# The first stage of a two-block kernel, rearranged by pairs of feature blocks

## The chip, the core and the metric

The kernel runs on one core of one Trainium2 chip. The metric is device time in microseconds (us), the median of several executions. A core has five engines: TensorE (PE; its weight loads, PEld, overlap the matmuls), VectorE (DVE), ScalarE (ACT), GpSimd (POOL) and SyncE (SP), which only issues transfers here. All data are 32-bit floats, so that a matmul of 512 columns shows as two records in the trace.

## What is computed

Two transformer-like blocks run one after the other. The change touches the beginning of the first one, which in the reference is (cut):

```python
sh, sc, gt = jnp.split(jax.nn.silu(c) @ w_ada[l] + b_ada[l], 3, axis=-1)
sh_c, sc_c, gt_c = jnp.split(jax.nn.silu(c_ctx) @ w_ada[l] + b_ada[l], 3, axis=-1)
h = rms_norm(x, norm_g[l]) * (1 + sc[:, None]) + sh[:, None]
hc = rms_norm(ctx, norm_g[l]) * (1 + sc_c) + sh_c
qa, ka, va, ga, qb, kb, vb, gb, qn, kn, vn, gn = split_proj(h @ w_in[l])
```

x has 1024 tokens and ctx 256, each of 1024 features. Tokens are normalised, scaled and shifted per feature (the modulation, whose shift and scale come from a product of a small vector with the large matrix w_ada), and then projected.

## The kernel before, in words

Tokens lie in ten tiles of 128 (NT; eight of x, two of ctx), features in eight blocks of 128 (KC). A kernel is a row of stages; each is a block in which the five engines run their own programs and wait for each other by semaphores, and at its end all engines meet. An engine works through its program in order, so that whatever stands behind a wait waits too.

`stage_begin` (L270) is the first stage. Its parts, with the lines of the profile:

- Transfers: SP issues small parameters (L286), the even token tiles (L288) and two of the four adaLN jobs (L290: 2 MB each, 512 columns of w_ada); POOL issues the odd tiles (L301), ACT the two other jobs (L333). When all four jobs have landed, SP loads the first two chunks of w_in (L203), and POOL the rest of the constants (L304).
- Norm: ACT squares and sums each tile (`square`, L313), in two groups of five (HALF). DVE and ACT make the reciprocal root of a group (L368, L221, L222, L225 to L228), and DVE scales each tile (L373).
- Turning: PE transposes a scaled tile, eight transposes in two PSUM banks (`turn`, L400); DVE copies the first four feature blocks to hT (`put`, L360), ACT the last four (`keep`, L322).
- Modulation: for each job PE makes rows (`rows`, L263), DVE copies them (`keep_rows`, L356), PE turns them into columns (`columns`, L413). When all four are done, DVE adds bias and gain in two small steps (L381, L382). Then DVE (five feature blocks, L389) and ACT (three, L345) modulate all of hT in place, in three spans of tokens.
- Ten filler matmuls (`keep_busy`, L255; 20 records) stand on PE between the columns and the first projection.
- One unit of the projection (BEGUN = 1): eight matmuls of 512 columns (L432), for token tile 0, with chunk 0 of w_in.

The second stage, `stage_project_turned`, does the attention's first projection: ten units of 512 columns (one for each token tile), then ten copies of 256 columns with chunk 1. Its matmuls are at L1003. The first `ahead` units (BEGUN of them) have been made before, and PE only signals them. A unit is squared by ACT (L1079), normalised by DVE (L1174 to L1184), rotated by POOL (L1276 to L1285), and transposed by PE (L956) four units later. Four PSUM banks, 0, 1, 6 and 7, hold units in turn, so that unit 4 needs the bank of unit 0: PE waits until unit 0 has been normalised (`bank_read`). ACT loads its table at the stage's start (L1030).

The order of work on every engine is written out by hand; no planner sets it.

Of the kernel before, what the change touches and what calls it, by code (L numbers as in the profile page):

```python
# [266 lines left out]
BEGUN = 1  # L267


def stage_begin(pr, t, const_src, x_rows, loads, ada_src):  # L270
# [4 lines left out]
    JOBS = 4  # L275
    ORDER = (0, 2, 3, 1)
    HALF = NT // 2
    SOON = P + 2
    cols = ps[:, 6, 0:32].rearrange("p (b w) -> p b w", w=2)
    spans = [(0, 0, BANK), (0, BANK, SEQ), (1, SEQ, SEQ + CTX)]  # L280
    by_dve, by_act = range(0, 5), range(5, KC)
    with nc.Block() as block:
        @block.sync
        def _(sp):
            for n, (dst, src) in enumerate(loads):
                sp.dma_start(dst, src).then_inc(*S["params_in"].inc(16))  # L286
            for i in range(0, NT, 2):
                sp.dma_start(big[:, i, :], x_rows(i)).then_inc(*S[f"x_in_{i}"].inc(16))  # L288
            for n in range(2):
                sp.dma_start(adaw[:, n], ada_src(n)).then_inc(*S[f"ada_in_{n}"].inc(16))  # L290
            for n in range(JOBS):
                sp.wait_ge(*S[f"ada_in_{n}"](16))
            for i in range(SLOTS):
                pr.load(sp, i)

        @block.gpsimd
        def _(pool):
            pool.memset(cs[:], 0.0).then_inc(*S["cs_zero"].inc())
            pool.dma_start(t["const"][:, 0:SOON], const_src[:, 0:SOON]).then_inc(*S["const_in"].inc(16))
            for i in range(1, NT, 2):  # L300
                pool.dma_start(big[:, i, :], x_rows(i)).then_inc(*S[f"x_odd_in_{i}"].inc(16))  # L301
            for n in range(JOBS):
                pool.wait_ge(*S[f"ada_in_{n}"](16))
# [4 lines left out]
        def _(act):  # L308
            step = chained(act, S["act"])

            def square(i):
                act.wait_ge(*S[f"x_odd_in_{i}" if i % 2 else f"x_in_{i}"](16))
                step(act.activation(junk[:, 0:D], big[:, i, :], ACT.Square, accum_out=ssq[:, i:i + 1]))  # L313

            def root(g):
                act.wait_ge(*S["v_ready"](g + 1))
                at = slice(g * HALF, (g + 1) * HALF)
                pr.rsqrt_act(act, step, rs[:, at], ssq[:, at]).then_inc(*S["e_ready"].inc())

            def keep(i):  # L320
                act.wait_ge(*S["turned_1"](i + 1))
                act.activation(hT[:, 4:8, i * P:(i + 1) * P], ps[:, 2 * (i % 2) + 1, :].rearrange("p (k n) -> p k n", k=4),  # L322
                               ACT.Copy).then_inc(*S["kept_1"].inc())

# [5 lines left out]
            for i in range(HALF):  # L330
                square(i)
            for n in range(2, JOBS):
                act.dma_start(adaw[:, n], ada_src(n)).then_inc(*S[f"ada_in_{n}"].inc(16))  # L333
            root(0)
            for i in range(HALF):
                square(HALF + i)
                keep(i)
            root(1)
            for i in range(HALF, NT):
                keep(i)  # L340
            act.wait_ge(*S["mod_ready"](1))
            act.wait_ge(*S["kept_1"](NT))
            for w, a, b in spans:
                for k in by_act:
                    ins = act.activation(hT[:, k, a:b], hT[:, k, a:b], ACT.Identity, scale=mod[:, 0, 8 + k, w:w + 1], bias=mod[:, 0, k, w:w + 1])  # L345
                ins.then_inc(*S["modulated_act"].inc())

        @block.vector
        def _(dve):
            step = chained(dve, S["dve"])  # L350

            def keep_rows(j):
                dve.wait_ge(*S["rows_done"](j + 1))
                if j >= 2:
                    dve.wait_ge(*S["cols_done"](j - 1))
                dve.tensor_copy(row[:, j % 2, :], ps[:, 4 + j % 2, :]).then_inc(*S["rows_kept"].inc())  # L356

            def put(i):
                dve.wait_ge(*S["turned_0"](i + 1))
                dve.tensor_copy(hT[:, 0:4, i * P:(i + 1) * P], ps[:, 2 * (i % 2), :].rearrange("p (k n) -> p k n", k=4))\  # L360
                   .then_inc(*S["kept_0"].inc())

            dve.wait_ge(*S["params_in"](16 * len(loads)))
            parameters_dve(pr, dve, step, 0, t)
            for g in range(2):
                at = slice(g * HALF, (g + 1) * HALF)
                dve.wait_ge(*S["act"](HALF + g * (HALF + 1)))
# [4 lines left out]
                for i in range(g * HALF, (g + 1) * HALF):  # L372
                    dve.tensor_scalar(big[:, i, :], big[:, i, :], rs[:, i:i + 1], None, ALU.mult).then_inc(*S["xn_ready"].inc())  # L373
                    if i % HALF:
                        put(i - 1)
                put((g + 1) * HALF - 1)
            for j in range(JOBS):
                keep_rows(j)
            dve.wait_ge(*S["cols_done"](JOBS))
            m0 = mod[:, 0, 0:16, :]  # L380
            step(dve.tensor_tensor(m0, cols, spread(mods[:, 0, 8:24], [P, 16, 2], 2), ALU.add))  # L381
            dve.scalar_tensor_tensor(out=mod[:, 0, 8:16, :], in0=mod[:, 0, 8:16, :], scalar=1.0, in1=spread(mods[:, 0, 0:8], [P, 8, 2], 2),  # L382
                                     op0=ALU.add, op1=ALU.mult).then_inc(*S["mod_ready"].inc())
            dve.wait_ge(*S["mod_ready"](1))
            dve.wait_ge(*S["kept_0"](NT))
            dve.wait_ge(*S["kept_1"](NT))
            for w, a, b in spans:
                for k in by_dve:
                    ins = dve.tensor_scalar(hT[:, k, a:b], hT[:, k, a:b], mod[:, 0, 8 + k, w:w + 1], mod[:, 0, k, w:w + 1], ALU.mult, ALU.add)  # L389
                ins.then_inc(*S["modulated_dve"].inc())  # L390

        @block.tensor
        def _(pe):
            def turn(i):
                pe.wait_ge(*S["xn_ready"](i + 1))
                for h in range(2):
                    if i >= 2:
                        pe.wait_ge(*S[f"kept_{h}"](i - 1))
                    for k in range(4):
                        mm = pe.transpose(ps[:, 2 * (i % 2) + h, k * P:(k + 1) * P],  # L400
# [3 lines left out]
            def rows(j):  # L404
                pe.wait_ge(*S[f"ada_in_{ORDER[j]}"](16))
                if j >= 2:
# [3907 lines left out]
```

## Time and profile before

| | us |
|---|---|
| median of 3 executions | 3650.55 (3649.99 to 3651.01) |
| the profiled execution, its own time | 3654.28 |
| its span (first to last instruction) | 3652.5 |
| PE busy | 3533.3 (97% of the span) |
| DVE, ACT, POOL busy | 2282.5, 1269.1, 1044.2 |

The page of the profile gives busy time and groups of instructions for the whole span; the trace behind it is read by views: windows (busy time of each engine in a stretch, the granted TensorE clock and what the transfers did), the timeline of one engine, groups by line, and one line's instructions. Each time starts from the span's start. A line of a timeline merges neighbours of one kind: start, length to the end of the last one, and the count.

### The profile page before, as it was taken

The numbers are of one execution on the slowest core, as the hardware profiler recorded it, in microseconds if no ns is written. First come the engines' busy times: TensorE is split into PE (matmuls) and PEld (weight loads), VectorE is DVE, ScalarE is ACT, GpSimd is POOL, SyncE is SP. The second block draws the span as 40 slices with busy tenths as digits, with TensorE's granted clock in tenths as the row PEclk, the third lists the DMA queues.
The fourth block names the chain that finished last, engine by engine and source line by source line (L and its number), as shares of the span: only waits on it lengthen the run. The fifth ranks groups of instructions, "written<-read, shape, count | busy, mean of one in ns | idle before, by whom it ended". The sixth has DMA issues, their size and how long they took to land. (4 is left out here: it accounts for less than half of the span.)

```text
span 3652.5 us, 53885 instructions
## 1 busy us (share of the span) xinstructions
PE 3533.3 (97%) x20756; PEld 2540.0 (70%) x20756; DVE 2282.5 (62%) x4223; ACT 1269.1 (35%) x2394; POOL 1044.2 (29%) x981
## 2 busy tenths in 40 slices
PE   7999998999999999989999999999998999999999
PEld 4656556789754655567897468555655588888888
DVE  4277454765675377557656661675548777894488
ACT  3255434632632255446426221674232311001100
POOL 2400064666541400256665330002224200000000
PEclk9999999999999999999999999999999999999999
DMA  5101142001112101110011221000000377552254
GB/s 199 49 18 42 59 153 93 2 8 52 37 61 92 50 18 41 61 36 1 1 47 49 88 74 58 3 22 24 24 24 19 113 273 264 184 179 98 92 184 161
DMA packets 142267, 279.01 MB, mean 76 GB/s; under 512 B 5728, under 2 KB 50784, under 8 KB 139584
## 3 DMA queue, kind: packets, MB, share of 16 engines
q1 hardware_dynamic: 114848, 221.89, 17.5%
q10 hardware_dynamic: 25872, 47.71, 3.7%
q0 software_dynamic: 1296, 5.97, 0.4%
q8 instruction: 168, 2.75, 0.3%
q14 instruction: 83, 0.68, 0.1%
HBM read 231.52 MB, written 44.04 MB: 75 GB/s over the span
## 5 line engine op out<-in xcount | busy, mean ns | idle before, releaser
L1003 PE MATMUL ps<-ring,hT 128*128 128x512 f32 (+3 forms) x1296 | 375.8, 446 | 9.6 <-DVE nrm_b L1184 4.4
L1003 PEld LDWEIGHTS ps<-ring,hT 128*128 128x128 f32 x1296 | 217.9, 191 | 145.9 <-issue 122.9
L1544 DVE TENSOR_REDUCE stat_a<-ps 128x1 f32<-128x1280 f32 (+1 forms) x144 | 190.7, 1365 | 153.9 <-PE ps L1388 153.9
L1442 PE MATMUL ps<-hT,ring 128*128 128x512 f32 (+1 forms) x640 | 280.2, 551 | 0.0
L1753 POOL TENSOR_TENSOR P_b<-P_b,stat_b 128x1280 f32<-128x1280 f32 (+1 forms) x108 | 227.8, 2130 | 174.6 <-DVE stat_b L1769 135.6
L2842 ACT ACTIVATE hid<-hid 128x1024 f32<-128x1024 f32 x32 | 33.8, 1057 | 482.5 <-DVE hid L2889 427.7
L1484 ACT ACTIVATE YT<-ps,stat_a 128x1280 f32<-128x1280 f32 (+1 forms) x144 | 176.5, 1231 | 25.4 <-DVE stat_a L1544 25.4
L2669 PE MATMUL ps<-Y 128*128 128x256 f32 x768 | 171.1, 379 | 0.9 <-DVE Y L2654 0.5
L1528 POOL COPY rb_a<-stat_a 128x64 f32<-128x64 f32 x72 | 14.6, 236 | 538.8 <-DVE YT L1557 538.8
L2669 PEld LDWEIGHTS ps<-Y 128*128 128x128 f32 x768 | 145.8, 190 | 21.3 <-issue 1.5
L1413 PEld LDWEIGHTS ps<-const,YT 128*128 128x128 f32 x656 | 71.6, 142 | 97.3 <-issue 86.5
L1672 PE MATMUL ps<-const,P_b 128*128 128x128 f32 x984 | 130.5, 279 | 5.9 <-POOL P_b L1753 4.5
L1726 ACT ACTIVATE P_b<-ps,stat_b 128x1280 f32<-128x1280 f32 (+1 forms) x108 | 132.8, 1236 | 3.9 <-DVE stat_b L1784 2.8
L1442 PEld LDWEIGHTS ps<-hT,ring 128*128 128x128 f32 x640 | 106.3, 191 | 39.3 <-issue 36.3
L1716 ACT ACTIVATE PT_b<-ps 128x512 f32<-128x512 f32 x146 | 82.0, 596 | 146.1 <-PE ps L1672 146.1
L3125 PE MATMUL ps<-hT,ring 128*128 128x348 f32 (+1 forms) x384 | 129.4, 466 | 0.0
L1672 PEld LDWEIGHTS ps<-const,P_b 128*128 128x128 f32 x984 | 106.1, 141 | 32.0 <-issue 24.4
L3409 POOL TENSOR_SCALAR aU_ssd<-const,sc_ssd 128x128 f32<-128x128 f32 x64 | 44.5, 712 | 282.2 <-DVE sc_ssd L3425 229.7
L1635 PE MATMUL ps<-qk_b 64*128 64x512 f32 (+1 forms) x590 | 119.6, 532 | 4.5 <-ACT P_b L1726 2.6
L1683 PE MATMUL ps<-PT_b,v_b 128*64 128x128 f32 x1968 | 120.1, 276 | 3.5 <-ACT PT_b L1716 1.8
L1683 PEld LDWEIGHTS ps<-PT_b,v_b 128*64 128x64 f32 x1968 | 107.0, 137 | 13.1 <-issue 9.4
L2669 PE MATMUL ps<-hT,ring 128*128 128x256 f32 x512 | 115.7, 379 | 0.0
(612 smaller groups left out, 8141.8 us busy)
## 6 DMA issues: line engine op xcount, KB each, us to landing
ring<-in_w_up SPq DMA_DIRECT2D x16, 2048.0 KB, 9.1
ring<-down_sums SPq DMA_DIRECT2D x16, 2048.0 KB, 8.3
ring<-in_w_in SPq DMA_DIRECT2D x14, 2048.0 KB, 8.1
ring<-in_w_down SPq DMA_DIRECT2D x12, 2048.0 KB, 7.9
adaw_b<-in_w_ada SPq DMA_DIRECT2D x16, 1024.0 KB, 5.2
ring<-in_w_out SPq DMA_DIRECT2D x6, 2048.0 KB, 7.9
Wd<-in_w_down ACTq DMA_DIRECT2D x11, 1024.0 KB, 7.3
down_sums<-Wd ACTq DMA_DIRECT2D x11, 1024.0 KB, 7.2
```

Of the source, the lines that this page charges most:

```text
L1003: mm = pe.matmul(ps[:, bank(n), 0:hi - lo], hT[:, k, t * P:(t + 1) * P], w[:, k, lo:hi], start=(k == 0), stop=(k == KC - 1))
L1442: mm = pe.matmul(ps[:, GB, 0:hi - lo], pr.view(i0 + c)[:, k, b % 4 * P:(b % 4 + 1) * P], hT[:, k, lo:hi], start=(k == 0), stop=(k == KC - 1))
L1484: act.activation(dst, scored_at(i, m), ACT.Exp, bias=st[:, i % 4, m:m + 1], accum_out=st[:, i % 4, 2 + m:3 + m])\
L1544: dve.tensor_reduce(st[:, i % 4, m:m + 1], scored_at(i, m), AX, ALU.max, negate=True)\
L1635: return pe.matmul(flat[:, at:at + width], qk[r, u["qb"], u["qt"] * P:(u["qt"] + 1) * P], qk[r, u["kb"], key:key + width], start=True, sto ...
L1672: mm = pe.transpose(ps[:, bank, (i - lo) * P:(i - lo + 1) * P], weights(p, e)[:, b * P:(b + 1) * P], ident)
L1683: mm = pe.matmul(O_AT[64 * e:64 * e + 64, :], V[:, key, u["v0"] + e * HD:u["v0"] + (e + 1) * HD], turned(p, e * nk[p] + b, e * nk[p] + b + ...
L1716: eng.activation(dst, src, ACT.Copy).then_inc(*S["pT_kept_act"].inc())
L1726: act.activation(weights(p, e), scored_at(p, e), ACT.Exp, bias=st[:, p % 8, e:e + 1], accum_out=st[:, p % 8, 2 + e:3 + e]).then_inc(*S["ex ...
L1753: pool.tensor_tensor(weights(p, e), weights(p, e), st[:, p % 8, 4 + e:5 + e].to_broadcast([P, nk[p] * P]), ALU.mult)\
L2669: mm = pe.matmul(pr.ps[:, bank, at], a[:, k, :], b[:, k, :], start=(k == 0), stop=(k == 3))
L3125: mm = pe.matmul(ps[:, dense_bank(u), 0:hi - lo], w[:, k, (b % 4) * P:(b % 4 + 1) * P], hT[:, k, lo:hi], start=(k == 0), stop=(k == KC - 1))
```

## The change

The first stage becomes one loop over four jobs; a job is a pair of feature blocks. BEGUN becomes 4.

- An adaLN job now fetches what one pair needs: 256 columns of shift and 256 of scale, in two transfers of 1 MB, all on SP's queue. Behind each job stand a quarter of chunk 0 of w_in (the pair's rows, 512 KB) and then two token tiles. Tiles 0 to 3 come first; ACT issues no transfers any more.
- Tiles are grouped 4, 2, 2, 2. For each group ACT squares, takes the root, copies the turned tiles, waits for the pair's modulation (`modulate_when`) and modulates one feature block of the first 512 tokens; only then come the squares of the next group. DVE does the like: norm, put, row copy, three small steps (`modulation`), one feature block. The remaining spans of tokens are modulated after the loop.
- PE adds, for each of four token tiles, the pair's share of the projection (`gather`: two of eight matmuls) in banks 0, 1, 6 and 7, and the next two tiles and the next job stand between these shares. The fillers are gone. Rows are made in bank 4 alone, columns in bank 5; tiles from the fifth on use banks 2 and 3 alone.

```diff
-BEGUN = 1
+BEGUN = 4
+BEGUN_BANKS = (0, 1, 6, 7)
-    JOBS = 4
-    ORDER = (0, 2, 3, 1)
-    HALF = NT // 2
+    JOBS = KC // 2
+    GROUPS = [range(0, 4), range(4, 6), range(6, 8), range(8, NT)]
+    def turn_bank(i, h):
+        return 2 * (i % 2) + h if i < 4 else 2 + h
+    def modulate_when(eng, j):
+        eng.wait_ge(*S["mod_ready"](j + 1))
+        for h in range(2):
+            eng.wait_ge(*S[f"kept_{h}"](4))
...
         def _(sp):
-            for i in range(0, NT, 2):
+            for i in (0, 2):
                 sp.dma_start(big[:, i, :], x_rows(i)).then_inc(*S[f"x_in_{i}"].inc(16))
-            for n in range(2):
-                sp.dma_start(adaw[:, n], ada_src(n)).then_inc(*S[f"ada_in_{n}"].inc(16))
-            for n in range(JOBS):
-                sp.wait_ge(*S[f"ada_in_{n}"](16))
-            for i in range(SLOTS):
+            for j in range(JOBS):
+                for part in range(2):
+                    sp.dma_start(adaw[:, j, :, part * 2 * P:(part + 1) * 2 * P], ada_src(part, j)).then_inc(*S[f"ada_in_{j}"].inc(16))
+                w = sp.dma_start(pr.view(0)[:, 2 * j:2 * j + 2, :], w_src(j))
+                if j < JOBS - 1:
+                    w.then_inc(*S[W_IN[j]].inc(16))
+                    for i in GROUPS[j + 1]:
+                        sp.dma_start(big[:, i, :], x_rows(i)).then_inc(*S[f"x_in_{i}"].inc(16))
+                else:
+                    w.then_inc(pr.loaded[0], 16)
+            for i in range(1, SLOTS):
                 pr.load(sp, i)
...
         def _(act):
-            for n in range(2, JOBS):
-                act.dma_start(adaw[:, n], ada_src(n)).then_inc(*S[f"ada_in_{n}"].inc(16))
...
+            for g in range(JOBS):
+                for i in GROUPS[g]:
+                    square(i)
+                root(g)
+                for i in GROUPS[g]:
+                    keep(i)
+                modulate_when(act, g)
+                modulate(2 * g + 1, first).then_inc(*S["modulated_act"].inc())
...
+            for j in range(JOBS):
+                for where in later:
+                    ins = modulate(2 * j + 1, where)
...
         def _(dve):
+            for j in range(JOBS):
+                norm(j)
+                dve.wait_ge(*S["rows_done"](j + 1))
+                dve.tensor_copy(row[:, j % 2, :], ps[:, 4, :]).then_inc(*S["rows_kept"].inc())
+                modulation(j)
+                modulate_when(dve, j)
+                modulate(2 * j, first).then_inc(*S["modulated_dve"].inc())
...
         def _(pe):
+            def gather(j, u):
+                if u == 0:
...
+                    pe.wait_ge(*S["modulated_dve"](j + 1))
+                    pe.wait_ge(*S["modulated_act"](j + 1))
+                for k in (2 * j, 2 * j + 1):
+                    pe.matmul(ps[:, BEGUN_BANKS[u], :], hT[:, k, u * P:(u + 1) * P], w[:, k, :], start=(k == 0), stop=(k == KC - 1))
...
-            keep_busy(pr, pe, 7, ident, 10)
-            for u in range(BEGUN):
-                for k in range(KC):
-                    pe.matmul(ps[:, u, :], hT[:, k, u * P:(u + 1) * P], w[:, k, :], start=(k == 0), stop=(k == KC - 1))
+            for i in GROUPS[0]:
+                turn(i)
+            rows(0)
+            columns(0)
+            for j in range(JOBS - 1):
+                i0, i1 = GROUPS[j + 1]
+                gather(j, 0)
+                gather(j, 1)
+                turn(i0)
+                rows(j + 1)
+                gather(j, 2)
+                turn(i1)
+                gather(j, 3)
+                columns(j + 1)
+            for u in range(BEGUN):
+                gather(JOBS - 1, u)
```

## Rows read from the trace of the kernel before

**Rows 1.** Windows; per engine busy us (instructions), then granted clock, DMA share, GB/s.

```profile
0.00:15.00 15.00, 0.00 (x0) 0.00 (x0) 0.98 (x10) 8.32 (x13) 3.85 (x11) 1.00 0.83 313
25.50:30.00 4.50, 0.00 (x0) 0.00 (x0) 1.75 (x8) 2.80 (x8) 0.00 (x0) 0.90 1.04 386
30.00:35.80 5.80, 5.76 (x27) 5.76 (x28) 4.55 (x7) 1.54 (x3) 0.00 (x0) 0.50 1.04 386
36.00:58.60 22.60, 21.99 (x146) 11.98 (x144) 10.79 (x23) 7.07 (x12) 0.53 (x1) 1.00 0.65 233
59.10:164.50 105.40, 105.33 (x384) 65.92 (x384) 31.63 (x70) 24.40 (x51) 58.10 (x80) 1.00 0.06 21
```

**Rows 2.** Timeline of PE, first stage: start, us, engine, line, operation [idle before].

```profile
18.74 6.71 PE L400 MATMUL ps<-const,YT 128*128 128x128 f32 x40 [18.74 <-DVE YT L373]
30.04 7.42 PE L400 MATMUL ps<-const,YT 128*128 128x128 f32 x40 [4.59 <-DVE YT L373]
37.39 3.64 PE L263 MATMUL ps<-adaw,cs 128*32 128x512 f32 x32
...
46.64 1.95 PE L413 MATMUL ps<-const,row 128*128 128x2 f32 x16
48.44 2.48 PE L255 MATMUL ps<-const 128*128 128x128 f32 x20
51.53 7.11 PE L432 MATMUL ps<-ring,hT 128*128 128x512 f32 x16 [0.61 <-DVE hT L389]
```

**Rows 3.** Timeline of PE, second stage.

```profile
59.11 27.70 PE L1003 MATMUL ps<-ring,hT 128*128 128x512 f32 x64 [0.48 <-PEq L282]
86.66 1.04 PE L956 MATMUL ps<-const,rot_a 128*128 128x128 f32 x8
87.53 7.03 PE L1003 MATMUL ps<-ring,hT 128*128 128x512 f32 x16
```

**Rows 4.** Timeline of ACT: the fourth square, and the second stage's start.

```profile
12.88 1.06 ACT L313 ACTIVATE junk<-YT 128x1024 f32<-128x1024 f32 x1
13.84 0.19 ACT L313 ACTIVATION_READ_ACCUMULATOR junk<-YT 128x1 f32 x1
...
58.90 1.28 ACT L1030 ACT_TABLE_LOAD   x1 [4.03 <-PEq L282]
```

**Rows 5.** Timeline of DVE: a group's norm, a job's copy, the small steps, unit 0's normalisation.

```profile
27.47 0.17 DVE L368 TENSOR_SCALAR ssq<-ssq 128x5 f32<-128x5 f32 x1 [1.82 <-ACT junk L313]
...
29.23 1.42 DVE L373 TENSOR_SCALAR YT<-YT,rs 128x1024 f32<-128x1024 f32 x2
...
39.38 0.69 DVE L356 COPY row<-ps 128x512 f32<-128x512 f32 x1 [1.63 <-PE ps L263]
...
48.62 0.19 DVE L381 TENSOR_TENSOR mod<-ps,mods 128x32 f32<-128x32 f32 x1 [1.16 <-PE ps L413]
...
49.06 6.27 DVE L389 TENSOR_SCALAR hT<-hT,mod 128x512 f32<-128x512 f32 x15
...
63.15 0.69 DVE L1184 TENSOR_TENSOR nrm_a<-ps,st_a 128x512 f32<-128x512 f32 x1
```

**Rows 6.** Timeline of POOL: the end of unit 0's rotation.

```profile
67.95 2.76 POOL L1285 TENSOR_TENSOR rot_a<-nrm_a,tmp_a 128x256 f32<-128x256 f32 x4
```

**Rows 7.** Line L400 from 18.7 to 22, then from 36: ns min/median/max.

```profile
L400 PE MATMUL ps<-const,YT x16: 411/421/448, 18.7 to 22.0; 128*128 128x128 f32 x16
...
L400 PE MATMUL ps<-const,YT x14: 272/273/401, 35.6 to 37.2; 128*128 128x128 f32 x14
```

**Rows 8.** Groups by line and form, 36 to 59: busy us, mean ns, idle before.

```profile
L345 ACT ACTIVATE hT<-hT,mod 128x512 f32<-128x512 f32 x6 | 4.3, 802 | 11.0 <-DVE mod L382 11.0
```

**Rows 9.** Page, DMA issues of a later stage: KB each, median us to landing.

```profile
adaw_b<-in_w_ada SPq DMA_DIRECT2D x16, 1024.0 KB, 5.2
```

**Rows 10.** Windows about a later fall of the clock, columns as in the first group.

```profile
2025.90:2029.20 3.30, 1.33 (x3) 0.68 (x4) 3.30 (x2) 0.12 (x1) 3.30 (x2) 1.00 0.49 190
2029.30:2032.60 3.30, 3.30 (x6) 1.24 (x5) 2.24 (x4) 1.34 (x4) 3.30 (x3) 0.50 0.00 0
```

More of the change, by code:

```diff
@@ L264, in modulation_rows, with stage_begin @@
     return mm
-BEGUN = 1
-def stage_begin(pr, t, const_src, x_rows, loads, ada_src):
+BEGUN = 4
+BEGUN_BANKS = (0, 1, 6, 7)
+def stage_begin(pr, t, const_src, x_rows, loads, ada_src, w_src):
     nc, S, ps = pr.nc, pr.S, pr.ps
@@ L350, in _, with norm @@
             step = chained(dve, S["dve"])
[L352 to L356, printed above, removed]
             def put(i):
                 dve.wait_ge(*S["turned_0"](i + 1))
-                dve.tensor_copy(hT[:, 0:4, i * P:(i + 1) * P], ps[:, 2 * (i % 2), :].rearrange("p (k n) -> p k n", k=4))\
+                dve.tensor_copy(hT[:, 0:4, i * P:(i + 1) * P], ps[:, turn_bank(i, 0), :].rearrange("p (k n) -> p k n", k=4))\
                    .then_inc(*S["kept_0"].inc())
[L363 to L367, printed above, removed]
+            def norm(g):
+                at = slice(GROUPS[g][0], GROUPS[g][-1] + 1)
+                dve.wait_ge(*S["squares"](GROUPS[g][-1] + 1))
                 dve.tensor_scalar(ssq[:, at], ssq[:, at], 1.0 / D, EPS, ALU.mult, ALU.add).then_inc(*S["v_ready"].inc())
@@ L379, in _ @@
[L379 to L384, printed above, removed]
+                put(GROUPS[g][-1])
@@ new lines, in modulate @@
+            def modulate(k, where):
+                w, a, b = where
+                return dve.tensor_scalar(hT[:, k, a:b], hT[:, k, a:b], scale[:, k, w:w + 1], shift[:, k, w:w + 1], ALU.mult, ALU.add)
+            dve.wait_ge(*S["params_in"](16 * len(loads)))
+            parameters_dve(pr, dve, step, 0, t)
+            for j in range(JOBS):
+                norm(j)
[4 more added lines that the diff above has]
+                modulate(2 * j, first).then_inc(*S["modulated_dve"].inc())
@@ L385, in _ @@
             dve.wait_ge(*S["kept_0"](NT))
             dve.wait_ge(*S["kept_1"](NT))
[L387 to L390, printed above, removed]
+            for j in range(JOBS):
+                for where in later:
+                    ins = modulate(2 * j, where)
+            ins.then_inc(*S["modulated_dve"].inc())
@@ L392, in _ @@
         @block.tensor
         def _(pe):
+            w = pr.view(0)
             def turn(i):
```

87 lines of the change are left out of this document (42 added, 45 removed).

## The prediction, made before the changed kernel was run

> **What bounds the kernel now.** I read the windows first, then the chain of work on each engine in the first 165 us. Over the whole span PE is busy for 97% of the time on the page, so what can be won lies where it idles. The windows [rows 1] split the start in two. In stage_begin TensorE does little and the transfers are the limit: in 25.5 to 30.0 PE has no busy time while the DMA engines are full (share 1.04, 386 GB/s), and the four adaLN jobs (the large weights) arrive last. Only from about 36 us on does PE pace the stage: modulation rows (37.39), columns, filler matmuls (48.44), one projection unit (51.53, 7.11 us) [rows 2]. The next stage is another matter: PE is busy for 105.33 of 105.40 us [rows 1], so each matmul that moves out of it shortens it, as long as no wait takes its place.
>
> **What the change takes out of the second stage.** Units 1 to 3 of the attention projection move ahead. 64 records took 27.70 us, 0.433 each [rows 3]; three units of 16 records are 48 x 0.43 = 20.6 us. In their place comes a wait. PE's first matmul there is now unit 4, whose bank is that of unit 0, and it waits until unit 0 is normalised. That chain started with ACT's table load at 58.90 [rows 4] and ended with DVE's normalisation at 63.15 + 0.69 = 63.84 [rows 5]; PE began at 59.11 [rows 3]. It ran under units 1 to 3 before, and without this cover it costs 63.9 - 59.1 = 4.8 us. After that PE stays the slowest: POOL's rotation of a unit goes from that end to 67.95 + 2.76 = 70.71, 6.9 us [rows 6]; PE's unit with its transposes is 16 x 0.43 + 0.87 (86.66 to 87.53 [rows 3]) = 7.7. Followed through all ten units, POOL's last rotated x tiles come within 0.4 us of delaying PE, no more. So the second stage gets shorter by 20.6 - 4.8 = 15.8; I take 16 (the start at 59.11 already held 0.2 of hand-over).
>
> **What the change does to the first stage.** Everything now runs in one loop over four pairs of feature blocks. The important edit is the order on ACT and DVE: both wait for the columns of pair j (modulate_when) before they take the squares and the norm of the next two token tiles, and behind that wait stand all of these tiles' squares, roots, copies. PE's transposes wait for them, the next job's row copy stands on DVE behind the second tile's copy, and the next columns wait for that. The loop is therefore a closed chain.
>
> First round: four squares end at 13.84 + 0.19 = 14.03 [rows 4]. From the squares' end to the first scaled tile is 29.23 - 27.47 = 1.76 [rows 5], 0.25 less where ACT has no copy in front; from there to the first transpose 30.04 - 29.23 = 0.81 [rows 2, 5]. So PE starts at 16.4 (it was 18.74 [rows 2]), cold: 0.421 us a transpose instead of 0.273 [rows 7], 1.7 us a tile instead of 0.9. Four tiles end at about 22.5 if the clock rises as early after the start as it did. Then rows (37.39 to DVE's copy at 39.38 = 2.0 [rows 2, 5]), copy and hand-over 0.75, columns 1.1 (half of 1.95 [rows 2] and the hand-over), three small DVE steps 0.56 (two steps were 49.06 - 48.62 = 0.44 [rows 5]). The first modulation starts at 22.5 + 2.0 + 0.75 + 1.1 + 0.56 = 26.9.
>
> One period, from modulation to modulation: ACT's modulation 0.70 (802 ns long [rows 8], the next can start 0.1 earlier); two squares 2.35 (12.88 to 14.03 is 1.15 [rows 4], with the hand-over); norm 1.55; first tile scaled and handed over 0.81; its transposes 0.9; rows 1.74 (half of 3.64 [rows 2], less the tail); third unit's part, 4 records, 1.72; second tile's transposes 0.9; fourth unit's part 1.72; columns 1.1; DVE steps 0.56. Sum 14.05; I take 14.15. The first two parts (3.44 us after the modulation) lie beside squares and norm and have 1.1 us to spare. Three periods: the last modulation at 26.9 + 42.45 = 69.35. Then ACT's 0.8 + 0.1, sixteen records 6.9, a tail of 0.2: PE ends at 77.3. Before, it ended at 51.53 + 7.11 = 58.64 [rows 2]. The first stage gets longer by 18.7.
>
> **Edits that cost nothing here, and their cover.** *Transfers:* the pieces that must land are 16.2 MB (5.2 of tiles, 8.4 of adaLN weights, 2.1 of projection weights, 0.5 small); 4.7 MB move in the first 15 us (313 GB/s [rows 1]), the rest at 386 by 45, and the fourth adaLN job has landed near 47; PE reaches its rows at 26.9 + 28.3 + 6.3 = 61.5. 14 us cover the finer pieces, the move of two jobs from ACT's queue to SP's (ACT loses two issues of about 0.5), and tiles queued behind weights on SP. The upper bound of the finer pieces is 5.2 us for each 1 MB as if it came alone [rows 9]: 42 us for adaLN, 20 for the rest, landing at about 65, 3.5 beyond the cover. I take 47, since queued transfers ran at 386. *POOL* issues the rest of the constants after the jobs, 8 us later than before; it is first read by the rotation, after 80. *SP* loads the second chunk behind all this; it is needed 40 us into the next stage. *Later spans:* eight modulations on each engine lie beside the last 6.9 us of matmuls; ACT's need about 5. *Single bank pair for tiles 4 to 9:* the second tile comes 3.5 us after the first, whose copies take 0.7.
>
> *The filler matmuls* (2.48 us, 48.44 [rows 2]) go. They lay beside the modulation and took nothing from the path, but they kept PE at work. In the loop PE now rests about 1.5 us between columns and the next matmul, after 0.9 us of columns that stream two columns each.
>
> **The clock.** Between 25.5 and 30.0 PE did nothing, and the granted clock was 0.50 for the next 5.8 us, 1.00 later [rows 1]. The 5 us rest between PE's end in the first stage and unit 4 in the second will do the same: half clock for 3.3 [rows 10] to 5.8 us [rows 1] after the restart, of which half is lost, 1.7 to 2.9, or 0 if the clock stays; I take 2, nearer to the rows. Inside the loop the bound below is 0, since PE is busy for four fifths of it. The nearest row for a fall is a stretch of 3.3 us with PE busy for 1.33, followed by one at 0.50 that was busy throughout [rows 10]: 1.7 us lost. The loop's rests are shorter (1.5 against 2.0), so I take one such loss, partly covered by the 1.1 to spare: 1.3.
>
> **Sum.** 18.7 - 16.0 + 2.0 + 1.3 = +6.0 us. Against the profiled execution (3654.28; span 3652.5) that is 3660.3; the runs' median is 3.7 below the profiled one, so 3650.55 + 6.0 = 3656.5. A measurement of this kernel can tell about 0.2%, 7.3 us, from no change: forecast no measurable change, on the slow side.
>
> **Where a page speaks otherwise.** The cold transposes at 18.7 to 22 took 421 ns, and those near 36, the clock having risen again with little but transposes running since 30.0, 273 ns [rows 1, 7]: here transposes raise the clock. The Trainium skill, "TensorE: Matmul & The Clock Gate", Part 4, says that transposes do not count as busy for the clock in the same way. By that, the first four tiles and the first rows and parts would all run cold; the rows speak against it.
>
> **Rivals.**
> (a) *The clock falls in most rounds.* Place: columns, DVE steps and modulation, where PE has 2.4 us almost without streaming and no filler. Price: 1.7 to 2.9 of loss a round; three rounds have 1.1 of cover, the last has none: 3 x 1.8 + 2.9 = 8.3 at most in place of 1.3, or with the clock at half throughout 6.7 a period and 6.9 at the end, 27. It decides from two rounds on. For it: the stretch in [rows 10]. Against it: the rests are shorter. Time 3658 to 3664, at the extreme 3677. Slower.
> (b) *The squares and norm hide.* If PE alone set the period (four parts 6.9, two tiles 1.8, rows 1.74, columns 0.9: 11.3), the stage would end 8.5 us earlier: 3648. Against it: ACT's program has the squares behind the modulation. It passes the edge of 0.2%, 3643.2, only with no loss of clock (3.3) and a warm first round (2) besides.
> (c) *Transfers late*, as bounded above: +3.5, 3660. For it: the stage is limited by transfers today. Against it: 14 us of cover.
> (d) *Transposes leave the clock low*, as a mechanism of this kernel: the first round starts its modulation 2.5 us later and its first two parts take twice as long, 3.4 less 1.1: +4, 3660.
>
> **How the numbers follow.** Forecast (3652 to 3659) 0.50; (a) 0.33; (b) 0.07; (c) 0.05; (d) 0.05. Slower by over 0.2%: (a), (c), (d) beyond 3657.9, less what of them falls below it, and the upper edge of the forecast: 0.42. Faster: the lucky part of (b) and a little more: 0.05. Within: 0.53. The range takes in (b)'s middle and all of (a) but its extreme: 3648 to 3667, with 3 us for periods longer than the sum's. The forecast's own: 3652 to 3659.
>
> **What would show it.** Right: PE's first transpose near 16.4; modulations 14 us apart, at about 27, 41, 55, 69; PE's last matmul of the stage near 77 and 5 us without one after it; the second stage's PE work 85 instead of 105. Wrong: a period of 11 (rival b), adaLN landings that PE waits for (c), granted clock 0.50 in several rounds (a), cold records after 24 us (d).

## The result and the profile after

The changed kernel takes 3655.74 us (median of 20 executions, 3652.61 to 3658.29), the kernel before 3650.56 beside it (20 executions, 3646.22 to 3653.86): a ratio of 1.0016 [1.0009, 1.0023], 5.2 us slower by the medians. The forecast was 6.0 us slower, 3656.5 us in a range of 3652 to 3659, and it held. It took 0.2% (7.3 us) for the least that a measurement of this kernel tells from no change; with 20 executions the interval lies wholly above 1, so the change made the kernel slower, by less than that 0.2%. The profiled execution took 3654.04 us with a span of 3652.3.

Single executions differ by some us through falls of the clock far behind the change: the two profiled executions, 3654.28 us for the kernel before and 3654.04 for the changed one, are alike in time, and behind the third stage the first was at half clock for 49.7 us in all, the second for 33.4. So the traces are compared at one early point, the first matmul of the third stage, in all that follows "the third stage". These are the timelines of PE, first before, then after (start, length to the end of the last one, engine, line, operation, count [idle before]). Lines behind the first stage have moved by 43.

```profile
165.38 1.36 PE L1388 MATMUL ps<-qk_a 32*128 32x128 f32 x16 [0.94 <-PEq L898]
```

```profile
16.60 5.95 PE L431 MATMUL ps<-const,YT 128*128 128x128 f32 x32 [16.60 <-DVE YT L388]
...
27.73 5.37 PE L456 MATMUL ps<-ring,hT 128*128 128x512 f32 x8 [1.46 <-ACT hT L349]
...
42.58 3.67 PE L456 MATMUL ps<-ring,hT 128*128 128x512 f32 x8 [1.46 <-ACT hT L349]
47.02 1.09 PE L431 MATMUL ps<-const,YT 128*128 128x128 f32 x8 [0.77 <-DVE YT L388]
48.04 1.92 PE L263 MATMUL ps<-adaw,cs 128*32 128x512 f32 x16
49.90 1.98 PE L456 MATMUL ps<-ring,hT 128*128 128x512 f32 x4
51.72 1.04 PE L431 MATMUL ps<-const,YT 128*128 128x128 f32 x8
52.59 1.88 PE L456 MATMUL ps<-ring,hT 128*128 128x512 f32 x4
54.31 0.95 PE L444 MATMUL ps<-const,row 128*128 128x2 f32 x8
56.74 3.67 PE L456 MATMUL ps<-ring,hT 128*128 128x512 f32 x8 [1.48 <-DVE hT L403]
...
70.86 7.11 PE L456 MATMUL ps<-ring,hT 128*128 128x512 f32 x16 [1.46 <-ACT hT L349]
83.23 8.55 PE L1046 MATMUL ps<-ring,hT 128*128 128x512 f32 x16 [5.26 <-DVE nrm_a L1227]
...
92.49 7.03 PE L1046 MATMUL ps<-ring,hT 128*128 128x512 f32 x16
...
170.34 1.36 PE L1431 MATMUL ps<-qk_a 32*128 32x128 f32 x16 [0.94 <-PEq L941]
```

The third stage begins 170.34 - 165.38 = 4.96 us later, nearly the whole 5.18 between the medians. One round of the loop stands between 42.58 and 56.74: two shares, a tile that waits 0.77 for its norm, rows, a third share, a tile, a fourth share, columns, and 1.48 of rest until the modulation is done. Behind the loop PE ends at 77.97 (58.64 before [rows 2]), rests 5.26, and runs unit 4 in 8.55, the next in 7.03.

ScalarE shows the order that makes the period. Timeline of ACT: a modulation, the first of the two squares behind it, the next modulation and the last; then DVE's row copy between the second and the third.

```profile
41.62 0.81 ACT L349 ACTIVATE hT<-hT,mod 128x512 f32<-128x512 f32 x1 [2.37 <-DVE mod L398]
42.34 1.04 ACT L335 ACTIVATE junk<-YT 128x1024 f32<-128x1024 f32 x1
...
55.76 0.81 ACT L349 ACTIVATE hT<-hT,mod 128x512 f32<-128x512 f32 x1 [2.37 <-DVE mod L398]
...
69.91 5.60 ACT L349 ACTIVATE hT<-hT,mod 128x512 f32<-128x512 f32 x9 [2.37 <-DVE mod L398]
```

```profile
52.96 0.68 DVE L410 COPY row<-ps 128x512 f32<-128x512 f32 x1
```

The trace can be followed around once from 41.62. The squares start 0.72 later and take 2.37; root, scaling and hand-over take 2.31, up to PE's tile at 47.02; then PE's tile 1.02, rows 1.86, share 1.82, tile 0.87 and share 1.72, up to the columns at 54.31; columns and DVE's small steps 1.45. The sum is 14.14, the next modulation at 55.76. The row copy is done at 53.64, before PE is through with the fourth share, so in this kernel it lies beside the chain.

The first modulation starts at 26.77, the others at 41.62, 55.76 and 69.91: periods of 14.85, 14.14 and 14.15. The first is longer by a fall of the clock: its first two shares took 5.37 instead of 3.67, and of these 1.7 us 1.0 was covered. Windows (busy us of PE, PEld, DVE, ACT, POOL with counts, granted clock, DMA share, GB/s):

```profile
28.10:31.40 3.30, 3.30 (x5) 1.33 (x4) 0.86 (x6) 2.08 (x6) 0.00 (x0) 0.50 1.04 374
...
42.60:56.70 14.10, 11.89 (x56) 5.98 (x56) 5.16 (x14) 4.56 (x10) 0.53 (x1) 1.00 0.74 251
...
78.00:83.20 5.20, 0.00 (x0) 0.00 (x0) 2.27 (x8) 2.80 (x5) 0.00 (x0) 0.95 0.00 0
83.30:86.00 2.70, 2.70 (x4) 1.15 (x5) 2.00 (x5) 0.92 (x3) 2.62 (x4) 0.50 0.00 0
86.10:168.00 81.90, 81.90 (x329) 55.19 (x328) 29.01 (x58) 20.31 (x42) 55.49 (x76) 1.00 0.07 26
```

The clock is at 0.50 in two stretches only, after the rest of the first round and after the rest between the stages.

### The profile page after: what moved, and what is told of

Same layout as the page of the kernel before. It is cut to its first block and busy times, and to the rows that moved or that the text cites. A ratio compares the mean times of both kernels' runs of the same rounds, so it can differ in the third digit from the quotient of the medians.

```text
span 3652.3 us, 53889 instructions
## 1 busy us (share of the span) xinstructions
PE 3526.4 (97%) x20736; PEld 2533.2 (69%) x20736; DVE 2287.4 (63%) x4240; ACT 1271.9 (35%) x2401; POOL 1043.0 (29%) x978
## 5 line engine op out<-in xcount | busy, mean ns | idle before, releaser
L1046 PE MATMUL ps<-ring,hT 128*128 128x512 f32 (+3 forms) x1248 | 355.1, 440 | 14.9 <-DVE nrm_a L1227 6.5
L1046 PEld LDWEIGHTS ps<-ring,hT 128*128 128x128 f32 x1248 | 208.6, 191 | 139.9 <-issue 109.7
```

The source lines that it names most:

```text
L1046: mm = pe.matmul(ps[:, bank(n), 0:hi - lo], hT[:, k, t * P:(t + 1) * P], w[:, k, lo:hi], start=(k == 0), stop=(k == KC - 1))
```

## The experiments

All read the same four points, and the time from the first share to the third stage: the first share starts anywhere from 26.62 to 28.54, though the edits change little of what runs before it, so small differences at the third stage are to be read from there. "Half" is the time at half clock from the first modulation to the third stage, read from the granted clock of the trace. Where no ratio is given, there is one profiled execution, and the verdict is read from the third stage.

| kernel | first share | last share done | first own unit of stage 2 | third stage | from first share | half |
|---|---|---|---|---|---|---|
| after | 27.73 | 77.97 | 83.23 | 170.34 | 142.61 | 6.8 |
| three units | 27.02 | 78.06 | 78.81 | 171.35 | 144.33 | 17.1 |
| one unit | 27.82 | 70.43 | 71.77 | 179.87 | 152.05 | 20.5 |
| norm ahead | 28.54 | 77.73 | 82.98 | 170.67 | 142.13 | 10.2 |
| fillers | 26.62 | 76.15 | 83.23 | 169.27 | 142.65 | 0 |
| late job | 27.63 | 77.87 | 83.14 | 170.51 | 142.88 | 6.8 |
| reorder, four | 27.10 | 70.41 | 75.67 | 164.42 | 137.32 | 10.2 |
| reorder, three | 27.67 | 64.09 | 65.65 | 158.18 | 130.51 | 3.4 |
| fillers after signal | 27.16 | 76.69 | 82.61 | 168.20 | 141.04 | 0 |
| three units, fillers | 28.00 | 74.30 | 75.07 | 167.60 | 139.60 | 0 |
| one unit, fillers | 26.77 | 64.34 | 67.48 | 175.44 | 148.67 | 3.4 |

### Three units instead of four

```diff
-BEGUN = 4
-BEGUN_BANKS = (0, 1, 6, 7)
+BEGUN = 3
+BEGUN_BANKS = (0, 1, 6)
-                gather(j, 3)
```

> The changed kernel with three units made ahead instead of four (the fourth share of each pair is left to the second stage). My theory: the second stage's first matmuls (unit 3) then cover the normalisation of unit 0, so the 5.26 us without a matmul and the fall of the clock behind it (1.5 us) go, while one unit of 6.87 us comes back there. In the first stage the row copy stands behind the second tile's copy and hides 1.1 of the 1.72 us of a share, so that a period shrinks only by 0.6, and the last shares by 1.72: 3.5 in all. Third stage's first matmul at 166.5 to 167.2 (170.34 in the changed kernel, 165.38 before). Rival, PE's work alone sets the stages and waits are hidden: 6.87 moves from one stage to the other and nothing changes, 170.3. Rival, the clock in the loop is what costs: stays at 170 or above.

Ratio 1.0018 [1.0008, 1.0028]; third stage 171.35, more than 4 us later than expected. Timeline of PE, then windows:

```profile
38.85 1.05 PE L444 MATMUL ps<-const,row 128*128 128x2 f32 x8 [0.94 <-DVE row L410]
41.36 5.08 PE L456 MATMUL ps<-ring,hT 128*128 128x512 f32 x8 [1.46 <-ACT hT L349]
...
70.98 7.08 PE L456 MATMUL ps<-ring,hT 128*128 128x512 f32 x12 [1.46 <-ACT hT L349]
78.81 13.97 PE L1045 MATMUL ps<-ring,hT 128*128 128x512 f32 x32 [0.75 <-PEq L296]
```

```profile
37.90:40.70 2.80, 1.06 (x9) 0.97 (x8) 1.58 (x6) 0.90 (x2) 0.00 (x0) 1.00 1.02 374
40.80:44.20 3.40, 2.84 (x4) 1.32 (x5) 0.32 (x3) 3.01 (x7) 0.00 (x0) 0.50 1.09 348
```

The rest of 5.26 is gone as expected (0.75), and so is the fall behind it. But without the fourth share there is a second rest, 0.94 before the columns, and the clock falls in every round: the first two shares take 5.37, 5.08 and 6.57 instead of 3.67, the last three 7.08. It is rival (a)'s mechanism, in another kernel than the one it was named for.

### One unit

The same edit with BEGUN = 1, and only `gather(j, 0)` left in the loop.

> The changed kernel with one unit made ahead, as before the change, in the new loop. My theory: this shows what the loop costs by itself. With one share between them, squares, norm, both tiles' transposes, rows and copies make a period of about 11.7 us; first modulation near 26.8, last near 61.8, PE's end near 64.7 (58.64 before), second stage as long as before (106), third stage's first matmul at 171.4, so the loop alone costs 6 us and the three further units bring nothing but 1 us. Rival, PE's work sets the loop: a period of 6.2 (one share, two tiles, rows, columns), PE's end at 49 or as the transfers allow, about 55, and 162 for the third stage.

Third stage 179.87, 8 us later than expected. The periods are 11.86, 13.50 and 13.50; in the two long ones the rows run slowly after a rest of 2.48:

```profile
39.68 1.96 PE L456 MATMUL ps<-ring,hT 128*128 128x512 f32 x4 [1.46 <-ACT hT L349]
44.12 1.41 PE L431 MATMUL ps<-const,YT 128*128 128x128 f32 x8 [2.48 <-DVE YT L388]
45.46 3.24 PE L263 MATMUL ps<-adaw,cs 128*32 128x512 f32 x16
```

In the period of 11.86 a fall lay on the share in front of that rest (3.58 instead of 1.96, the rest 0.86 instead of 2.48) and cost nothing. Both misses have one suspect, the clock; the last two experiments hold it.

### Squares and norm ahead of the modulation

```diff
             for g in range(JOBS):
                 for i in GROUPS[g]:
-                    square(i)
-                root(g)
-                for i in GROUPS[g]:
                     keep(i)
+                if g < JOBS - 1:
+                    for i in GROUPS[g + 1]:
+                        square(i)
+                    root(g + 1)
                 modulate_when(act, g)
```

The first group's squares and root stand ahead of the loop; DVE's part of the mean moves likewise.

> The changed kernel with ACT's squares and roots of the next two tiles, and DVE's mean for them, ahead of the wait for the pair's modulation instead of behind it. My theory: the wait of PE for the next tile after its first two shares (0.77 us a period) goes, the rest of the chain (rows, shares, copies, columns, steps, modulation) stays: periods of 13.4 instead of 14.15, third stage's first matmul near 168.0. Rival, the whole chain hangs on squares and norm: periods of 11.3, and 161.8. Rival, the wait is not on the path (transfers or clock are): 170.3 as in the changed kernel.

Third stage 170.67 instead of the expected 168.0. The tile's wait of 0.77 is gone, but the modulation now waits behind the squares and root, and the share's rest grows from 1.46 to 1.93. The periods are 15.33 (with a fall that nothing covers now: 5.37 instead of 3.67 for the two shares), 13.62 and 13.13. Moving the squares alone wins 0.5 to 1.0 a round, not the 2.8 of rival (b). In the first two rounds the chain is closed in another way: the squares now stand behind ACT's copy of the second tile, and DVE's mean of them stands ahead of the modulation's small steps. These are DVE's mean, which waits for the squares, and ACT's modulation, which follows root and squares without a gap:

```profile
55.98 0.17 DVE L387 TENSOR_SCALAR ssq<-ssq 128x2 f32<-128x2 f32 x1 [2.05 <-ACT junk L335]
```

```profile
56.53 0.80 ACT L349 ACTIVATE hT<-hT,mod 128x512 f32<-128x512 f32 x1
```

The round of 13.13, the last, has no squares; there PE still rests 1.45 between the columns and its next share.

### Fillers in the rests, and their place

Six idle 128x128 products ahead of each round's first share, and 22 at the second stage's start:

```diff
+                keep_busy(pr, pe, 2, ident, 6)
                 gather(j, 0)
...
+            if ahead == BEGUN:
+                keep_busy(pr, pe, 2, work["ident"], 22)
             for n, (kind, spec, ts) in enumerate(units):
```

> The changed kernel with filler matmuls on PE where it rests: 6 between the columns and the next pair's first share, 22 at the start of the second stage, in a bank that is free there. My theory of the clock's share: the granted clock stays at 1.00 in both places; the first period is 14.15 instead of 14.85, the second stage's first unit takes 7.0 instead of 8.55 us, third stage's first matmul at 168.2 instead of 170.34; the periods themselves stay 14.15, since the rests are waits for others. Rival (a), the clock is what makes the loop long: periods fall well below 14.1. Rival, fillers delay the path: above 170.3.

The clock stayed at 1.00 up to the third stage, the periods were 14.14 each, unit 4 took 7.13 instead of 8.55. But the third stage began at 169.27, 1.1 later than expected, and from the first share on (142.65 against 142.61) nothing was won:

```profile
76.44 5.15 PE L255 MATMUL ps<-const 128*128 128x128 f32 x44 [0.30 <-PEq L296]
83.23 7.13 PE L1050 MATMUL ps<-ring,hT 128*128 128x512 f32 x16 [1.64 <-DVE nrm_a L1231]
```

From the last share's end at 76.15 to unit 4 it is 7.1 instead of 5.3: the fillers stood on PE's queue ahead of the signals that release the normalisation. The repair puts the 22 behind those signals, at the first unit that PE makes itself (`if n == ahead == BEGUN:` inside the loop over the units):

> The changed kernel with idle 128x128 products on the TensorE again (6 ahead of each round's shares, 22 in the second stage), but those 22 now stand behind the signals for the first four units and no longer ahead of them. In the run that had them ahead, the third stage began at 169.27 us and the normalisation came some 1.5 us late. Theory (only the place of the 22 was wrong; the clock costs what the rows say): granted clock 1.00 through the first 170 us, rounds of 14.14 us, first whole unit of the second stage 7.1 us, its start 5.2 to 5.4 us after the first stage's last product, third stage at 167.5 to 168.0. Rival (the delay of 1.5 us had another source, the fillers are no use): third stage at 169 or later.

Ratio 1.0012 [1.0002, 1.0021]; clock 1.00, periods 14.14, unit 4 in 7.03, third stage 168.20, 0.2 above the expected range and below the rival's 169. Unit 4 starts 5.92 after the last share, not 5.3, since here the fillers end last (no wait behind them):

```profile
77.62 5.15 PE L255 MATMUL ps<-const 128*128 128x128 f32 x44 [0.93 <-PEq L296]
82.61 7.03 PE L1050 MATMUL ps<-ring,hT 128*128 128x512 f32 x16
```

So the place was at fault. From the first share to the third stage it is 141.0 here (168.20 - 27.16) and 142.6 in the changed kernel (170.34 - 27.73): 1.6 less, and 2.2 if the fillers' surplus of 0.66 is taken off. That is the 0.7 in the loop and the 1.5 behind the rest, by another way.

### The fourth job later

SP loads chunk 1 (1 MB) ahead of the fourth adaLN job, and POOL issues the rest of the constants after two jobs (at 26.98 instead of 48.32).

```diff
             for j in range(JOBS):
+                if j == JOBS - 1:
+                    pr.load(sp, 1)
                 for part in range(2):
...
-            for n in range(JOBS):
+            for n in range(JOBS - 2):
                 pool.wait_ge(*S[f"ada_in_{n}"](32))
```

> The changed kernel with 1.9 MB more ahead of the last adaLN job: chunk 1 of w_in before it on SP's queue, and the rest of the constants from POOL two jobs earlier. The fourth job lands some 5 us later, near 53 instead of 48. My theory: transfers are off the path by 14 us (PE reaches the fourth rows at 62.2), so the third stage's first matmul stays at 170.3, within 0.7 either way for the clock. Rival (c), transfers set the stage: 175.

Periods 14.85, 14.15, 14.14; third stage 170.51 against 170.34. The issues of the adaLN pieces (tile view; duration ns, then first and last start) in after and here:

```profile
L305 SPq DMA_DIRECT2D adaw<-in_w_ada x8: 434/1458/4912, 3.5 to 32.4; - x8
```

```profile
L307 SPq DMA_DIRECT2D adaw<-in_w_ada x8: 434/3174/4912, 3.5 to 38.9; - x8
```

The last piece is issued 6.5 us later, and nothing moves. The transfers are not on the path.

### Another order, with four units and with three

ACT and DVE make the norm of the next pair of tiles while PE still works on this pair's, and PE makes rows and columns early in the round and turns the tiles behind them:

```diff
                 gather(j, 0)
+                rows(j + 1)
                 gather(j, 1)
+                columns(j + 1)
                 turn(i0)
-                rows(j + 1)
                 gather(j, 2)
                 turn(i1)
                 gather(j, 3)
-                columns(j + 1)
...
+            squares(0)
+            root(0)
+            for i in GROUPS[0]:
+                keep(i)
+            squares(1)
+            root(1)
+            for j in range(JOBS):
+                squares(j + 1 if j else JOBS)
+                modulate_when(act, j)
+                modulate(2 * j + 1, first).then_inc(*S["modulated_act"].inc())
+                if j:
+                    keep(GROUPS[j][0])
+                    if j < JOBS - 1:
+                        root(j + 1)
+                    keep(GROUPS[j][1])
```

> The changed kernel with the loop opened: rows and columns of the next pair stand between the first shares of this one (share 0, rows, share 1, columns, tile, share 2, tile, share 3), squares and norm of a group one round ahead, so that the next pair's modulation lies beside shares and tiles. My theory (the closed chain through modulation, copies and columns is what makes the first stage long): periods of PE's work alone, about 11.5 instead of 14.15, PE's end of the first stage near 69 instead of 78; the stall of 5.3 and the clock loss at the second stage's start stay; third stage's first matmul near 161.5, 4 before the kernel before, 3647. Rival, the transfers take over as the limit: the fourth job lands at 48 and is needed at 52, so the periods stay near 14 or PE waits for the job: 165 to 170.

> The opened loop with three units made ahead: periods of about 9.8, PE's end of the first stage near 62.5, no stall and no fall of the clock at the second stage's start, third stage's first matmul at 155 to 158 against 165.38 before the change; device time 3641 to 3644, ratio 0.9975 or less. My theory says that the change's idea pays once the chain is open and the second stage's first unit still covers the normalisation. Rival, the transfers limit it: the fourth job, landing at 48.3, is needed at 48.9, tiles 8 and 9 at 44: PE waits for them and the third stage starts at 160 or later, 3646 or more.

With four units: ratio 0.9995 [0.9985, 1.0005], third stage 164.42. With three (no `gather(j, 3)`): 3642.24 us, ratio 0.9979 [0.9971, 0.9988], 8.5 us under the kernel before in the medians and 7.2 at the third stage. Its time lies in the expected 3641 to 3644; its third stage (158.18 for 155 to 158) and its last share (64.09 for 62.5) came later than expected, and its ratio is not the 0.9975 or less. The version with three units beats both kernels, by little. Its PE timeline and windows:

```profile
40.99 1.92 PE L263 MATMUL ps<-adaw,cs 128*32 128x512 f32 x16
...
50.79 1.92 PE L263 MATMUL ps<-adaw,cs 128*32 128x512 f32 x16
...
65.65 13.97 PE L1077 MATMUL ps<-ring,hT 128*128 128x512 f32 x32 [1.56 <-PEq L296]
```

```profile
28.70:32.00 3.30, 3.30 (x11) 0.60 (x13) 0.67 (x2) 2.30 (x4) 0.00 (x0) 0.50 1.06 362
32.10:64.00 31.90, 31.90 (x160) 16.70 (x152) 16.08 (x43) 12.71 (x24) 0.53 (x1) 1.00 0.68 230
```

A round is 9.80 and PE rests nowhere in it (31.90 of 31.90), so the closed chain is open and PE sets the period. Squares, rows and columns were moved together; what each is worth by itself is not shown, but for the squares ("norm ahead"). With four units a round is 11.52 and the rest between the stages is back, with a fall of 6.8 us behind it:

```profile
75.67 10.19 PE L1078 MATMUL ps<-ring,hT 128*128 128x512 f32 x16 [5.26 <-DVE nrm_a L1259]
```

The fourth unit costs 6.2 us at the third stage here (6.8 from the first share on): last share 6.3 later, rest 3.7 longer (5.26 against 1.56), clock 3.2 (10.19 - 7.03), less a unit of 6.95. A clock loss of 3.2, where the changed kernel's 1.5 was counted on, and a last share 1.4 us later than expected are why this run missed its 161.5 by 2.9.

### The misses again, with the clock held

Three units with fillers, in the PSUM bank that is free there: 6 ahead of the first share, 4 ahead of the columns. One unit likewise, with 10 more behind its share.

```diff
+                keep_busy(pr, pe, 7, ident, 6)
                 gather(j, 0)
                 gather(j, 1)
                 turn(i0)
                 rows(j + 1)
                 gather(j, 2)
                 turn(i1)
+                keep_busy(pr, pe, 7, ident, 4)
                 columns(j + 1)
```

> The kernel with three begun units again, with idle products in the rests: 4 ahead of each round's columns, 6 ahead of each round's first share, in a PSUM bank that is free there. Without them its third stage began at 171.35 us instead of the 166.5 to 167.2 expected, with rounds of 14.3, 14.1 and 15.6 us and the clock at half in each. Theory (the clock alone made that run miss): clock 1.00 through the loop, rounds of 13.6 us, last share done at 73 to 74, no rest of 5 us behind it, third stage at 166.0 to 167.2. Rival (something in VectorE's or ScalarE's order, not the clock, makes the rounds long with three units): rounds above 14 us although the clock is 1.00, third stage at 170 to 171.

> The kernel with one begun unit again, with idle products in the rests: 10 behind the round's only share, 4 ahead of the columns, 6 ahead of the share. Without them its rounds were 11.86, 13.50 and 13.50 us and the third stage began at 179.87. Theory (the clock made the long rounds): clock 1.00 through the loop, rounds of 11.7 to 11.9 us, last share done at 63.5 to 65, third stage at 171.5 to 173. Rival (the rounds are bound by something else): rounds of 13 us or more at full clock, third stage above 177.

Three units: ratio 1.0007 [0.9998, 1.0017], third stage 167.60, 0.4 above the expected range. Timeline of PE, one round, and windows at the place of the fall shown above:

```profile
38.01 1.06 PE L255 MATMUL ps<-const 128*128 128x128 f32 x8
39.12 1.05 PE L444 MATMUL ps<-const,row 128*128 128x2 f32 x8
40.03 1.58 PE L255 MATMUL ps<-const 128*128 128x128 f32 x12
41.63 3.67 PE L456 MATMUL ps<-ring,hT 128*128 128x512 f32 x8
```

```profile
37.90:41.60 3.70, 3.65 (x31) 3.28 (x29) 2.10 (x6) 1.53 (x3) 0.00 (x0) 1.00 1.05 375
41.70:45.30 3.60, 3.60 (x8) 1.34 (x8) 0.86 (x6) 2.38 (x6) 0.00 (x0) 1.00 1.09 349
```

The waits are as long as they were, only filled; the clock stays and the share takes 3.67 instead of 5.08. Rounds of 13.63, 13.67 and 13.61, as expected. The run started its first share 1.0 later than the one without fillers, so the clock's price there is 4.7 us (171.35 - 27.02 against 167.60 - 28.00). So the clock made that run miss: with the rests filled and nothing else moved, the rounds are as long as the chain makes them.

One unit: rounds of 11.87, 11.91 and 11.83 and the last share done at 64.34, as expected. The third stage, at 175.44, came 2.4 later than I gave it. The second stage started late and at half clock:

```profile
67.48 29.40 PE L1047 MATMUL ps<-ring,hT 128*128 128x512 f32 x64 [3.14 <-PEq L296]
```

ACT's modulation of the later spans started at 61.43 and took 5.60; the stage can't end before it, so PE rests 3.14, and the clock is at half for 3.4 us after that: the 64 records take 29.40, 27.70 in the kernel before [rows 3]. The expectation left at most 109.5 from the last share to the third stage, about what the run without fillers had taken (109.4); here it is 111.1. Without the fillers PE's last share was the late one, so the rest was only 1.34; the clock was at half there too, up to 75.5.

## Why the prediction was right

The mechanism was the one forecast, and the large terms came out within 0.2; the two terms of the clock, 1.3 and 2.0, were both taken too large, at 0.7 and 1.5. The measured terms add up to the difference at the third stage: 19.3 - 20.6 + 4.8 + 1.5 = +5.0.

- **The closed chain.** Forecast: modulations at 26.9 and every 14.15 us, last at 69.35. Measured: 26.77, 14.14 where the clock stood, last at 69.91. That the order makes the period is shown by the reordered kernels: with another order of the same work a round falls from 14.1 to 11.5 with four units, and from 13.6 (clock held) to 9.8 with three. The parts of the forecast period fit the trace too, as followed around above. Its sum was 14.05, though, and it took 14.15 without a reason for the 0.1. The row copy, which it names as a link, has 0.7 to spare with four units; it is a wait (0.94) with three.
- **First stage's end.** Forecast 77.3, and 1.3 for the clock in the loop, from one fall. Measured 77.97: one fall, 14.85 - 14.14 = 0.7. The sum's 18.7 + 1.3 is 20.0, against 77.97 - 58.64 = 19.3.
- **The new wait.** Forecast 4.8 beyond the hand-over that was there. Measured 5.26, less 0.48 [rows 3]: 4.8. The normalisation of unit 0 is the releaser on the row, as argued.
- **The clock behind that rest.** Forecast 2.0; unit 4 took 8.55 - 7.03 = 1.5 longer. In three runs with the same rest of 5.25 or 5.26 it cost 1.8 (late job), 2.1 (norm ahead) and 3.2 (reorder, four), so 2.0 was in the middle of what occurs, and the size in any one kernel could not be told.
- **The transfers.** Forecast: fourth job at 47, rows at 61.5. POOL, which waits for all four jobs, issued at 48.32; the rows came at 62.19. The late job showed the cover.
- **Second stage.** 83.23 to 170.34 is 87.11, from 59.11 to 165.38 106.27: 19.2 shorter, the 20.6 less the 1.5 of clock. That leaves nothing for POOL as a bound.

The rivals:

(a) *The clock in most rounds.* It didn't happen, but my reason against it was poor, and as far as that reason goes it was luck that the clock fell in one round of four and not in all. I compared the length of the rests; three units and one unit have rests of that kind too and fell in every round, for 4.7 us with three units. The rows show one difference. Ahead of the first share the columns have a rest on both sides, 0.81 or 0.82 and then 1.46, in all seven kernels without fillers, and so they have in the later rounds of three units, with 0.94 and 1.46 to 1.49; the clock fell in all ten. In the later rounds of after, norm ahead and late job the fourth share stands directly ahead of the columns, with only one rest of 1.45 to 1.93 behind them; it fell in none of nine. What it is about the second rest that matters is not settled. (The extreme of this rival was added wrongly: 3656.5 - 1.3 + 27 is 3682, not 3677; nothing hangs on it.) The nearest pair of rows: with three units PE was busy for 1.06 of 2.80 us ahead of a fall; in after it was for 1.42 of the 2.80 us just ahead of the shares at 42.58, and no fall followed:

```profile
39.70:42.50 2.80, 1.42 (x10) 1.05 (x8) 0.94 (x4) 0.88 (x2) 0.00 (x0) 1.00 1.08 354
```

The Trainium skill, "TensorE: Matmul & The Clock Gate", section "Loop structure matters more than you think", says that the loop nest decides whether matmuls stay warm. The traces agree, with the share ahead of the columns as the difference.

(b) *Squares and norm hide.* Refuted for this kernel by its period, and for the squares alone by "norm ahead". It takes the order of tiles, rows and columns too (11.5 a round), and then the first stage's shares end 7.6 us earlier than in the changed kernel, against (b)'s 8.5.

(c) *Transfers late.* Refuted by "late job".

(d) *Transposes leave the clock low.* Refuted. Line L431 of after from 16.5 to 18.4, then from 20 to 22.5, then the first modulation rows (ns min/median/max):

```profile
L431 PE MATMUL ps<-const,YT x9: 421/421/448, 16.6 to 18.3; 128*128 128x128 f32 x9
...
L431 PE MATMUL ps<-const,YT x18: 272/273/421, 19.6 to 22.3; 128*128 128x128 f32 x18
...
L263 PE MATMUL ps<-adaw,cs x16: 592/592/617, 22.5 to 23.8; 128*32 128x512 f32 x16
```

Nothing but transposes had run, they became fast within themselves, and the rows behind them took the 592 ns that they take later. The Trainium skill, "TensorE: Matmul & The Clock Gate", Part 4, says that the full clock does not engage for transposes. For these, of 32-bit data, the rows show that it did, and the measurement decides.

What the prediction did not weigh is how the fourth unit pays. With the clock held, the way from the first share to the third stage is 139.6 us with three units (167.60 - 28.00) and 141.0 with four (168.20 - 27.16): the fourth costs 1.4, or 0.7 without the fillers' surplus of 0.66. Its shares lengthen three rounds by 0.5 each and the last by 1.7, its rest is 5.1 longer (5.92 against 0.77), and it saves 6.95. Bringing a fourth unit forward meets the bank limit of the next stage, so its gain turns into the wait.

## What to carry to other kernels

When a loop makes one piece of work on four engines, follow the chain of waits once around: work that stands behind a wait on an in-order queue joins the period even if nothing needs it yet. Here another order was worth 2.6 us a round with four units and 3.8 with three, and moving the squares alone 0.5 to 1.0. Work brought forward pays only up to the buffers of the stage it comes from; here the unit that filled the last bank moved its own time into a wait. Judge the clock by where the rests fall, and if a result hangs on it, fill the rests with idle products, behind every signal that others wait for.

## What the hardware showed unexpectedly

- Short rests were enough for a fall. With three units, 0.94 and 1.46 us with 1.05 of two-column matmuls between them (0.81 and 1.46 ahead of the first) put the clock to 0.50 in all four rounds; the same rests filled with products kept 1.00 throughout. With a share directly ahead of the columns, a rest of 1.45 to 1.93 behind them was followed by no fall in nine rounds of three kernels. A fall could also lie where it cost nothing (one unit, first round).
- The same rest did not cost the same. After 5.25 or 5.26 us without a matmul, the half clock ended after 1.5 to 3.2 us of loss in four kernels.
- The queue's rate went with the row length of what it moved. DMA view of after, 0 to 60 us in 40 slices, GB/s:

```profile
GB/s 0 59 221 365 396 415 387 362 348 349 364 408 400 360 348 349 350 380 412 384 353 348 349 359 400 404 360 348 349 347 372 360 350 330 370 19 0 5 0 0
```

The stretches at 348 to 350 are adaLN weights, now in rows of 256 columns (1 KB; the 512 columns before, in rows of 2 KB, ran at 386 [rows 1]), and the humps of 400 to 415 are w_in and tiles behind them, in rows of 2 and 4 KB. The packets bear this out: from 21.0 to 25.5 us 1546 of 1550 are under 2 KB, at 349 GB/s; from 18.0 to 19.4, on the same queue, 140 of 156 are of 2 to 8 KB, at 410. That the length of a row is the cause, and not what else differs between these loads, was not tested by itself. The Trainium skill, "DMA: Bandwidth & Descriptors", section "Where 436 GB/s comes from", holds that about 358 GB/s of the memory binds for such loads. Here, with one core at work, slices of 400 to 415 are above that, and the measurement decides.
